# Mixing experts by 32 tokens and 4 slots, with replicated token rows, in a one-core encoder kernel

## The reference, cut to what matters

```
q = (xb @ wq) per head, RMS-normed                  # 8 heads of 256
s1, s2 = q1 @ k1.T, q2 @ k2.T                       # 128 keys each
v1, i1 = top_k(s1, 16);  v2, i2 = top_k(s2, 16)
sv, si = top_k(v1[:, None] + v2[None, :], 16)       # of 256 sums
expert = i1[si // 16] * 128 + i2[si % 16]           # one of 16384
g   = softmax(sv)
act = gelu(sum_d u[expert, d] * xb[d])
out = sum over 8 heads and 16 places of g * act * v[expert]
```

## Time and profile before

| | us |
|---|---|
| median of 3 runs | 3307.72 |
| lowest and highest run | 3305.47, 3307.9 |
| span of the profiled execution | 3302.0 |
| gather stage, first issue to the last mix | 587.3 to 3294.0 |

### The profile page before, as it was taken

The page is one execution under the profiler, slowest core; times in us unless marked ns, Lnnn a source line. Parts: engine busy times, 40 slices in busy tenths (PEclk is TensorE's granted clock), DMA queues, the critical chain, the costliest instruction groups (busy, mean ns, idle before and its releaser), DMA issues. The chain is left out here.

```text
span 3302.0 us, 33384 instructions
## 1 busy us (share of the span) xinstructions
PE 2886.4 (87%) x9454; PEld 1408.2 (43%) x9454; DVE 2218.7 (67%) x5274; ACT 2154.6 (65%) x7216; POOL 1392.2 (42%) x1135
## 2 busy tenths in 40 slices
PE   7999999888888888888898888888988898889886
PEld 5665455444434433444344344343443344434321
DVE  5687265776676667666766676667666766676665
ACT  3332143677777777777777777777777777777775
POOL 0000110455544555554455544544555445544553
PEclk9999999999999999999999999999999999999999
DMA  7232133999999999999999999999999999999997
GB/s 284 87 104 76 30 122 125 369 419 418 420 419 403 419 420 420 414 420 420 420 396 420 420 420 419 420 421 418 403 420 420 420 413 420 420 418 406 421 420 302
DMA packets 170079, 1190.91 MB, mean 361 GB/s; under 512 B 20058, under 2 KB 21498, under 8 KB 30242
## 3 DMA queue, kind: packets, MB, share of 16 engines
q0 software_dynamic: 155808, 1118.53, 82.1%
q1 hardware_dynamic: 14084, 70.23, 5.7%
HBM read 1179.42 MB, written 9.25 MB: 360 GB/s over the span
## 5 line engine op out<-in xcount | busy, mean ns | idle before, releaser
L929 PE MATMUL ps<-r_w,r_yT 128*128 128x512 f32 (+1 forms) x2712 | 1320.6, 622 | 256.2 <-ACT r_yT L1255 253.4
L604 POOL DMA_INDIRECT r_w<-in_peer_uv,gidx x678 | 860.5, 1269 | 880.3 <-PE ps L929 841.8
L1806 DVE SCALAR_TENSOR_TENSOR r_w<-r_w,r_qk 128x1024 f32<-128x1024 f32 x678 | 829.9, 1225 | 499.9 <-DMA r_w<-in_peer_uv,gidx 494.7
L929 PEld LDWEIGHTS ps<-r_w,r_yT 128*128 128x128 f32 (+1 forms) x2712 | 485.8, 192 | 1018.3 <-ACT r_yT L1255 600.8
L929 PE MATMUL ps<-r_yT 128*128 128x512 f32 (+1 forms) x904 | 443.7, 620 | 72.4 <-ACT r_yT L1255 70.1
L1247 ACT ACTIVATE mixc<-mixc 128x1 f32<-128x1 f32 x1056 | 207.8, 197 | 449.5 <-DVE r_w L1806 286.0
L1255 ACT ACTIVATE r_yT<-ident,mixc 128x128 f32<-128x128 f32 x1024 | 411.3, 402 | 33.2
L1252 ACT ACTIVATE mixc<-mixc 128x1 f32<-128x1 f32 x1056 | 408.9, 387 | 35.0
L1251 ACT ACTIVATE mixc<-mixc 128x1 f32<-128x1 f32 x1056 | 408.7, 387 | 33.8
L604 POOL DMA_INDIRECT r_yT<-in_peer_uv,gidx x226 | 298.5, 1321 | 269.4 <-PE ps L929 257.3
L1806 DVE SCALAR_TENSOR_TENSOR r_yT<-r_yT,r_qk 128x1024 f32<-128x1024 f32 x226 | 276.6, 1225 | 176.1 <-DMA r_yT<-in_peer_uv,gidx 175.9
(11 more groups left out here) (293 smaller groups left out, 2777.3 us busy)
## 6 DMA issues: line engine op xcount, KB each, us to landing
r_w<-in_ada_w SPq DMA_DIRECT2D x18, 1024.0 KB, 5.3
r_w<-in_peer_uv,gidx POOLq DMA_INDIRECT x678
r_w<-in_w_lin SPq DMA_DIRECT2D x16, 512.0 KB, 6.9
r_vo<-in_x_prompt SPq DMA_DIRECT2D x8, 512.0 KB, 7.2
r_qk<-in_ada_w SPq DMA_DIRECT2D x2, 2048.0 KB, 16.7
r_w<-in_w_out SPq DMA_DIRECT2D x2, 2048.0 KB, 8.9
r_w<-in_x_prompt SPq DMA_DIRECT2D x8, 512.0 KB, 3.5
x_dram<-r_w POOLq DMA_DIRECT2D x8, 512.0 KB, 3.4
```

The lines of the kernel that those rows point to most:

```text
L604: pool.indirect_dma_start(ring[i], None, table, bass.IndirectOffsetOnAxis(gidx_t[:, h, j:j + 1], 0)).then_inc(e_ld[i], 16)
L929: mm = nc.tensor.matmul(ps[0:r, 2 * p + c, :], diag[:, j % 4, 0:r], row[:, D + c * 512:D + (c + 1) * 512], start=h == 0 and j == 0, stop=h ...
L1806: V.scalar_tensor_tensor(ring[i][:, 0:D], ring[i][:, 0:D], 1.0, h2[:, t, :], ALU.mult, ALU.mult, accum_out=dots[:, i:i + 1]).then_inc(dot_ ...
```

## The change

A slot is now 32 tokens by 4 places of one head instead of 128 tokens by 1 place. The number of gathers (1056), their rows (128) and their size (8 KB) stay.

- Partition group k (of 32) holds place 4g+k of the same 32 tokens. For this the 32 token rows are repeated four times: `replicate` makes them with two matmuls against the constant `spread`, ScalarE copies them from PSUM (`copy_rows`) into one of two buffers `xrep`, and a buffer serves 4, 8 or 16 slots (`SETS`: the heads that are taken together for one group of 32 tokens).
- Places and gates must be moved to the right partitions: VectorE spreads them with a mask (`xi`, `xg`), TensorE sums them (`turn_places`, `turn_gates`, four calls each), VectorE converts the places (`copy_places`), ScalarE copies the gates (`copy_gates`).
- `mix` is four calls, each a diagonal 128x32 against 256 columns of v, into the four column groups of the array; the sum over four places falls out of it. There is one accumulator, so the first mix of a tile waits on `acc_free`.
- `weight` has five instructions instead of six; the factor of the tanh moves into the dot.
- The accumulator is laid out in 4 x 256 columns by 32-partition groups. The final steps therefore work on [128, 4, 256] (for the sample tile on [128, 1, 256]), the sum of squares over the four groups is made on TensorE (`sum_squares`), and x1 and y move in four DMAs each, with rows of 1 KB. The rows g2 and the final weights are loaded in 12 small DMAs.
- The table `ROUTE_AT` says at which slot the routing of each head begins, one head every 16 slots from the seventeenth on; six early heads (`FAST`) are routed in fewer slots.

The diff, cut to its core (the constants, the slots' order, the SyncE transfers of a tile's end, TensorE's new steps, ScalarE's weight, VectorE's places, gates, dot and final sum):

```diff
-K_ROUTE, K_GATE, K_W, K_FIN = 13, 2, 3, 3
+K_ROUTE, K_W, K_FIN = 14, 3, 5
+QUADS, NG = 4, 16
+QC = 256
+SETS = [((0,), (1,), (2, 3), (4, 5), (6, 7)), ((0, 1), (2, 3), (4, 5, 6, 7))] + [
+    ((0, 1, 2, 3), (4, 5, 6, 7))] * (NT - 3) + [((0,), (1,))]
+FAST = (2, 3, 12, 13, 14, 15)
+ROUTE_AT = {2: 2, 3: 10, 4: 22, 5: 37, 6: 53, 7: 69, 8: 85, 9: 101, 10: 116, 11: 132,
+            12: 146, 13: 154, 14: 162, 15: 170, 16: 180}
+ROUTE_AT.update({m: 180 + 16 * (m - 16) for m in range(17, (NT - 1) * HEADS + S_STEPS)})
...
-            return (t, h + 2, P) if h < HEADS - 2 else (t + 1, h + 2 - HEADS, rn)
+        slots, builds, first = [], [], []
+        for t in range(NT):
+            for heads_of in SETS[t]:
+                for q in range(QUADS if t < NT - 1 else 1):
+                    builds.append((t, q))
+                    first.append(len(slots))
+                    for h in heads_of:
+                        for c in range(4 * q, 4 * q + 4) if t < NT - 1 else range(NG):
+                            slots.append((t, h, q, c, len(builds) - 1, number(t, heads_of[-1])))
+        assert len(slots) == N_SLOTS
+        first.append(N_SLOTS)
+        spans = {}
+        for n, x in enumerate(slots):
+            spans.setdefault((x[0], x[2] // 2), []).append(n)
+        N_ROUTES = number(NT - 1, S_STEPS)
+
+        def routes(s):
+
+            return [m for m in range(2, N_ROUTES) if 0 <= s - ROUTE_AT[m] <= 20]
+
+        def build_at(s):
+
...
-            def finish(t, r, src, dst):
-                sp.dma_start(x1s[0:r], src).then_inc(x1_ld, 16)
+
+            def finish(t, nq, src, dst):
+                for c in range(4):
+                    sp.dma_start(x1s[c * DEC:(c + 1) * DEC, 0:nq, :],
+                                 src[:, c * QC:(c + 1) * QC].rearrange("(q j) n -> j q n", q=nq)).then_inc(x1_ld, 16)
                 sp.wait_ge(y_out, t + 1)
-                sp.dma_start(dst, h2[0:r, t, :]).then_inc(y_st, 16)
-
-            for t in range(NT - 2):
-                finish(t, P, x1_t[t], y_t[t])
-            sp.wait_ge(y_st, 16 * (NT - 2))
-            sp.dma_start(g2s, mod_dram[1, 5 * D:6 * D].partition_broadcast(DEC)).then_inc(g2_ld, 16)
-            finish(NT - 2, P, x1_t[NT - 2], y_t[NT - 2])
-            finish(NT - 1, DEC, x1_dram[SEQ:T], outs[1][0])
-            sp.wait_ge(y_st, 16 * NT)
+                for c in range(4):
+                    sp.dma_start(dst[:, c * QC:(c + 1) * QC].rearrange("(q j) n -> j q n", q=nq),
+                                 h2[c * DEC:(c + 1) * DEC, t, 0:nq * QC].rearrange("p (q n) -> p q n", q=nq)).then_inc(y_st, 16)
+
+            for t in range(NT - 1):
...
+            def turn_places(m):
+
+                pe.wait_ge(idx_x, m + 1)
+                if m:
+                    pe.wait_ge(gate_ready, m)
+                for k in range(4):
+                    mm = nc.tensor.matmul(ps[k * DEC:(k + 1) * DEC, 6, 16:32], sel32, xi[:, :, k:NG:4],
+                                          start=True, stop=True)
+                mm.then_inc(idx_t, 1)
+
+            def turn_gates(m):
+
+                pe.wait_ge(gate_x, m + 1)
+                pe.wait_ge(idx_ready, m + 1)
+                for k in range(4):
+                    mm = nc.tensor.matmul(ps[k * DEC:(k + 1) * DEC, 6, 32:48], sel32, xg[:, :, k:NG:4],
+                                          start=True, stop=True)
+                mm.then_inc(gate_t2, 1)
+
+            def replicate(b):
+
+                t, i = builds[b]
+                if b:
+                    pe.wait_ge(x_copy, b)
+                q = slice(i * DEC, (i + 1) * DEC)
                 for c in range(2):
-                    mm = nc.tensor.matmul(ps[0:r, 2 * p + c, :], diag[:, j % 4, 0:r], row[:, D + c * 512:D + (c + 1) * 512],
-                                          start=h == 0 and j == 0, stop=h == steps(r) - 1 and j == TOPK - 1)
+                    mm = nc.tensor.matmul(ps[:, 2 + c, :], spread[q, :],
+                                          h2[q, t, c * 512:(c + 1) * 512], start=True, stop=True)
+                mm.then_inc(x_rep, 1)
+
+            def mix(s):
+
+                t, h, q, _, _, _ = slots[s]
+                pe.wait_ge(dg_ready, s + 1)
+                if t and s == t * TILE_SLOTS:
+                    pe.wait_ge(acc_free, t)
+                row = ring[place[s]]
+                new, end = s == spans[t, q // 2][0], s == spans[t, q // 2][-1]
+                for c in range(4):
+                    mm = nc.tensor.matmul(ps[c * DEC:(c + 1) * DEC, q // 2, (q % 2) * QC:(q % 2 + 1) * QC], diag[:, s % 4, :],
+                                          row[:, D + c * QC:D + (c + 1) * QC], start=new, stop=end)
                 mm.then_inc(v_free, 1)
 
-            pe.wait_ge(kt_ld, 16)
...
-            def weight(t, h, r, j):
-
-                s = slot0(t, h) + j
+            def weight(s):
+
+                t, h, _, c, _, m = slots[s]
                 wch.base, wch.n = s * K_W, 0
-                i, d = j % 2, dots[:, place[s]:place[s] + 1]
+                i, d = s % 2, dots[:, place[s]:place[s] + 1]
+                if s == 0 or m != slots[s - 1][5]:
+                    act.wait_ge(gate_ready, m + 1)
                 act.wait_ge(dot_done, s + 1)
-                nc.scalar.activation(sq[:, i:i + 1], d, ACT.Square, scale=(TANH_K * GELU_C) ** 0.5)
-                act.wait_ge(v_free, s + 5)
-                nc.scalar.activation(kd[:, i:i + 1], d, ACT.Copy, scale=TANH_K)
-                wch.link(nc.scalar.activation(gd[:, i:i + 1], gate_t[:, h, j:j + 1], ACT.Copy, scale=d))
-                wch.link(nc.scalar.activation(th[:, i:i + 1], sq[:, i:i + 1], ACT.Tanh, scale=d, bias=kd[:, i:i + 1]))
+                wch.mark(nc.scalar.activation(sq[:, i:i + 1], d, ACT.Square, scale=GELU_C ** 0.5 / TANH_K))
+                nc.scalar.activation(gd[:, i:i + 1], gate_t[t % 2][:, h, c:c + 1], ACT.Copy, scale=d)
+                wch.need()
+                wch.link(nc.scalar.activation(th[:, i:i + 1], sq[:, i:i + 1], ACT.Tanh, scale=d, bias=d))
                 wch.link(nc.scalar.activation(wc[:, i:i + 1], th[:, i:i + 1], ACT.Identity, scale=gd[:, i:i + 1],
                                               bias=gd[:, i:i + 1]))
                 assert wch.n == K_W
-                nc.scalar.activation(diag[:, j % 4, 0:r], (ident if r == P else sel32)[:, 0:r], ACT.Copy,
+                act.wait_ge(v_free, RING + s - 3)
+                nc.scalar.activation(diag[:, s % 4, :], sel32, ACT.Copy,
                                      scale=wc[:, i:i + 1]).then_inc(dg_ready, 1)
+
+            def copy_gates(m):
+
+                t, h = tile_head(m)
+                act.wait_ge(gate_t2, m + 1)
+                nc.scalar.activation(gate_t[t % 2][:, h, :], ps[:, 6, 32:48], ACT.Copy).then_inc(gate_ready, 1)
+
+            def copy_rows(b):
+
+                act.wait_ge(x_rep, b + 1)
+                if b >= 2:
+                    act.wait_ge(dot_done, first[b - 1])
+                nc.scalar.activation(xrep[b % 2], ps[:, 2:4, :].rearrange("p b n -> p (b n)"), ACT.Copy).then_inc(x_copy, 1)
 
...
                 assert rc.n == K_ROUTE, rc.n
-                V.scalar_tensor_tensor(gidx_t[:, h, :], e12[:, half[0]], float(P), e12[:, half[1]],
-                                       ALU.mult, ALU.add).then_inc(idx_ready, 1)
-
-            def gates(m, h):
-                gc.base, gc.n = m * K_GATE, 0
+                V.tensor_tensor(xi, idxf.unsqueeze(1).broadcast_to([P, QUADS, NG]),
+                                jm.unsqueeze(2).broadcast_to([P, QUADS, NG]), ALU.mult).then_inc(idx_x, 1)
+
+            def copy_places(m):
+                t, h = tile_head(m)
+                dve.wait_ge(idx_t, m + 1)
+                V.tensor_copy(gidx_t[:, t % 2, h, :], ps[:, 6, 16:32]).then_inc(idx_ready, 1)
+
+            def gates(m):
                 dve.wait_ge(p_exp, m + 1)
-                gc.link(V.reciprocal(prs, psm))
-                gc.link(V.tensor_scalar(gate_t[:, h, :], pexp, prs, 0.5, ALU.mult, ALU.mult))
-                assert gc.n == K_GATE
-
-            def dot(t, h, j):
-                s = slot0(t, h) + j
-                i = place[s]
+                link(V.reciprocal(prs, psm))
+                if m:
+                    dve.wait_ge(gate_t2, m)
+                V.scalar_tensor_tensor(xg, pexp.unsqueeze(1).broadcast_to([P, QUADS, NG]), prs,
+                                       jmk.unsqueeze(2).broadcast_to([P, QUADS, NG]), ALU.mult, ALU.mult).then_inc(gate_x, 1)
+
+            def dot(s):
+                i, b = place[s], slots[s][4]
+                if s == first[b]:
+                    dve.wait_ge(x_copy, b + 1)
                 dve.wait_ge(e_ld[i], 16 * uses[s])
-                V.scalar_tensor_tensor(ring[i][:, 0:D], ring[i][:, 0:D], 1.0, h2[:, t, :], ALU.mult, ALU.mult,
+                V.scalar_tensor_tensor(ring[i][:, 0:D], ring[i][:, 0:D], TANH_K, xrep[b % 2], ALU.mult, ALU.mult,
```

(26 more changed lines are left out.)

421 lines of the change are left out of this document (238 added, 183 removed).

## The result

The changed kernel takes 3336.5 us (median of 4 runs, 3334.5 to 3337.8), the kernel before on the same chip 3306.6 (3303.8 to 3307.9): a ratio of 1.009, 95% interval 1.0076 to 1.0104. The forecast was 3309.7 with a range of 3298 to 3333. It missed on the slow side.

The account below looks back on a forecast made before the run. The gather stage was taken to be bound by DMA at 2.485 us per gather, one lagging engine setting the dots. Span 3302.0 - 1.3 + 4 - 2.7 + 2 = 3304.0, plus 5.7 to the median: 3309.7 us, range 3298 to 3333.

Parts of the forecast that it names:

- Step 1: Mixes on four column groups: about 0.6 us or 1.9 as now, below the 2.49 between mixes, so nothing in the stage.
- Step 2: Builds of replicated rows, two TensorE calls and a ScalarE copy per 4 to 16 gathers: hidden, cost 0.
- Step 3: Turning places and gates on TensorE: places reach GpSimd just in time, a miss of some us costs 0.
- the laggard: The one DMA engine that lags and sets the dots in the gather stage; its queue covers 22.8 us with 11 places.
- Rival D: GpSimd waits for late places at each of some 20 set borders, a few us each: 3330 to 3350; chance 0.05.
- Step 4: Program fetches in the gather stage: ScalarE's shrinking program moves the end by -1.3 us, TensorE's growing one costs 0.
- Step 5: Residual and output in 1 KB rows at the eight tile borders: +4 us, from 1.5 to 11.
- Step 6: Chain after the last dot, with smaller VectorE passes and a shorter mix: -2.7 us, from -1.7 to -3.0.
- Step 7: Start of the stage: first dot 6 us later, eleventh gather issued at about 621.5 instead of 618.37: +2 us, 0 to +4.
- A: Dips in the mean DMA share at tile borders do cost, and the shorter mix shrinks them: 3299 us; chance 0.15.
- B: TensorE's program fetches, on only two DMA engines, decide the stage once they grow: 3337 us; chance 0.10.
- C: Short mixes leave TensorE at 1.2 GHz, so queries stop gathers at the first tile borders: +14, 3324 us; chance 0.10.

Follow-up runs that it names:

- e13: Changed kernel with heads taken in pairs in all tiles from 1 on, one head routed every 16 slots: 3329.5 us, ratio 1.0059.
- e9: Kernel before with five ScalarE instructions per weight instead of six, the tanh factor moved into the dot: 3306.4 us, ratio 0.9996.
- e1: Changed kernel with three idle TensorE calls of 256 columns behind each mix: 3443.4 us, ratio 1.042.
- e4: Kernel before with two more TensorE calls of 8 columns behind each mix: 3308.3 us, ratio 1.0006.
- e3: Kernel before with residual load and output store each in four DMAs of 1 KB rows over all 128 partitions: 3309.8 us, ratio 1.0011.
- e11: Kernel before with only the residual's loads in blocks of 32 partitions by four rows of 1 KB, rows permuted: 3324.3 us, ratio 1.005.
- e6: Kernel before with residual loads and output stores in blocks of 32 partitions by four rows of 1 KB, rows permuted: 3324.0 us, ratio 1.0058.
- e15: Changed kernel with e13's pairs and the residual's loads over all 128 partitions in 1 KB rows, rows permuted: 3316.0 us, ratio 1.0024.
- e10: Kernel before with five idle VectorE passes of 1024 columns, about 6.3 us, ahead of the first dot: 3308.2 us, ratio 1.0001.
- e5: Changed kernel with two idle TensorE calls behind each mix, but none next to a query or a build: 3339.0 us, ratio 1.0103.
- e7: Changed kernel with tile 1's sample query moved to head 0 and head 2's routing begun at slot 3 instead of 2: 3332.8 us, ratio 1.0083.
- e12: Changed kernel with tile 1's sample query moved to head 0 and two idle calls behind mixes only in slots 3 to 109: 3332.0 us, ratio 1.0067.

## Why the prediction was wrong, step by step

**What bounds the kernel** was read rightly: the pace stayed at 2.49 us, dots wait for gathers, and the time is in the extras above the pace.

**Step 1, the column groups.** Right. A mix takes 0.64 us at the full clock and 1.08 at half, so the four groups run beside each other. It gained nothing in the stage, as forecast.

**Step 2, the replicated rows.** Held as to time: e13 has 16 builds per tile, twice as many as the changed kernel's later tiles, and is no slower.

**Step 3, places just in time.** This step failed. I checked when a head's places reach GpSimd and priced lateness at nothing, since the laggard's queue covers a few us. I looked at the regular distance of 16 slots, and not at heads 12 to 15, 8 slots apart, one of them (13) with the sample's query besides. There VectorE's wait for the gates takes its dots along (6.7 us at once, 10.0 in two waits), and the queue of 8 places is not deep enough: from 1020 to 1050 the DMA engines fall short. Price: 8.3 us instead of 0, of which e13 gives back 7.5. Rival D has this sign but not this place or size: it put it at every set's border.

**Step 4, the instruction streams.** The size came near by luck; the reason is not borne out. ScalarE's program did not shrink: the 909 activations that went are outweighed by waits that are now instructions of their own (1332 in the trace instead of 174), and the stage has 103 q14 packets, where it had 100 before. In e9, which drops the activation and adds no waits, it has 91. What changed is the size of the steps. Steps of 0.96 us now stand where a q14 packet passes (the queues of 2420 to 2423, and the dots on either side):

```profile
q14 instruction: 1, 0.01, 0.7%
```

```profile
2419.33 1.23 DVE L1934 SCALAR_TENSOR_TENSOR r_w<-r_w,r_vo 128x1024 f32<-128x1024 f32 x1 [0.39 <-DMA r_w<-in_peer_uv,gidx]
...
2422.78 1.23 DVE L1934 SCALAR_TENSOR_TENSOR r_w<-r_w,r_vo 128x1024 f32<-128x1024 f32 x1 [1.73 <-DMA r_w<-in_peer_uv,gidx]
```

They go with VectorE's program. Of the 24 steps of 0.90 to 1.02 us behind slot 60, 22 fall at places 51 to 66 when VectorE's records are counted modulo 128; in the kernel before the 28 steps of 0.62 to 0.75 us fall at places 56 to 82 of ScalarE's. e9 has 24 steps of 0.90 to 1.02 too. Why ScalarE's packets, as many as before, leave hardly a step in the changed kernel is open. And the slots outside the named ranges lose 2.7 us of extra, where I had -1.3, but that is inside the scatter: they have 25.9 here, 25.5 to 32.9 in the variants of the changed kernel (e1 left out), and 28.8 in the kernel before.

TensorE's packets are 99 in the stage (about 100 forecast); e4 shows in the kernel before that 31 more of them cost nothing that shows.

```profile
q8 instruction: 99, 1.62, 0.2%
```

**Step 5, rows of 1 KB.** The term that failed by most: +4 (1.5 to 11) forecast, 17.8 measured at the borders. I costed packet by packet, by size, and the size explains none of the borders: e3 has the same rows and the old borders (its total, +3.4 us, is no more than the +4). What costs is that each load writes into 32 partitions, four rows to each, while gathers run: e11 (loads alone) +16, e6 (loads and stores) +18, e15 (loads over 128 partitions) 13.4 back. By the traces that is 2.1 us (e11) and 2.2 us (e15 against e13) for each of the seven borders with a load of 512 KB; the changed kernel has 2.5 more at each. The earlier trace rows could not show this, for its 4 KB rows lie over 128 partitions. The Trainium skill ("DMA: Bandwidth & Descriptors", Specifications), which I weighed there, puts the line rate at transfers of 512 B and more. e3's borders agree, at 3.2 to 3.9 us extra with rows of 1 KB; that row speaks of size alone and says nothing of a block of 32 partitions.

**Step 6, the tail.** Right: -2.9 against -2.7. The first of the small passes, 0.42 us instead of 1.22:

```profile
3327.78 0.42 DVE L1945 TENSOR_TENSOR r_qk<-ps,r_wr 128x256 f32<-128x256 f32 x1 [2.68 <-PE ps L1000]
```

**Step 7, the start.** This term failed too: +2 forecast, 9.7 measured, 2.2 of it ahead of the first gather, so about 7. The issue behind the third mix comes 6.7 us later, not 3.1; the forecast left out the query that now stands ahead of this mix (6.31 us). But that this issue sets the loss is not borne out. e10 issues the same gather 34.5 us after its first, the changed kernel 35.5 and the kernel before 31.0, and e10 loses nothing; e5 issues at 35.5 as well, and its lateness at slot 16 is 610.9 instead of 614.6; e7 issues at 33.5 and gains nothing. The direct DMAs of 625 to 630 us are in no term of the prediction and in no experiment. The cause of the start's loss stays open. That a late first dot is covered was right (e10).

**The rivals.** A fell with its sign, for the kernel is slower; its premise got no run of its own. B fell by e4. C had its condition right, the clock stands at 0.50 for 78% of the stage, and its price, +14 us, wrong: e15 is only 7.6 us above the kernel before at a clock of 0.68, with the borders and most of tile 1 mended. At the start the clock may play a part.

**The sum of the miss.** On the span I forecast 3304.0, and it is 3333.9, 29.9 more: 13.8 in step 5 (17.8 - 4), 8.3 in step 3, 7.7 at the start (9.7 - 2, of it 2.2 ahead of the stage), 1.7 in slots 30 to 60, less 1.4 in the other slots and 0.2 at the tail. The first is shown by e11 and e15, the second by e13; the start is not explained. On the median the miss is 26.8, for the 5.7 us that I added between span and median is 2.6 in this kernel. The slots from 30 to 60 have no experiment of their own; in e13 and e15 they have 1.7 and 2.0 extra.

## What to carry to other kernels

Where gathers hold all DMA engines, the shape of a direct transfer beside them counts as well as its bytes and its row size: try it over 128 partitions, even if the layout wants blocks of 32 (e15 shows what that gives back, not a kernel with the right output). Look at the densest place of a schedule, not at its rule: four routings at half distance cost 8.3 us here, where the regular ones of e13 leave 2.5 extra against 1.7 before. And read GB/s beside the DMA share: here a share of 1.07 with 299 GB/s was contention, and in e12 a share of 0.71 with 266 GB/s was a queue that ran dry.

## What the runs showed of the hardware

- Loads in blocks of 32 partitions, 512 KB at a time, slow the gathers beside them by 2.1 to 2.2 us (e11, e15), 299 to 365 GB/s at a DMA share of 1.02 to 1.07 (the changed kernel, e11), and a gather's 8 KB packet takes 325 to 328 ns over such a border instead of 315. The same rows of 1 KB over 128 partitions cost nothing at the borders (e3, 406 GB/s, 316 ns) and +3.4 us (0.7 to 6.9) in all. The stores in blocks add nothing that shows (e6 against e11). Why is open: which DMA engines the block's packets go to, and the order of rows in DRAM, were not tried.
- Four matmul groups of 32 columns, 256 wide, take 0.64 us together at the full clock, 1.08 at half, where two of 512 over all columns took 1.92.
- With mixes this short the granted clock is 0.50 for 78% of the stage (mean 0.673 over the whole kernel), and between the gathers, at the borders and in e13's tile 1 this stage, bound by DMA, shows no loss from it.
- Steps that go with VectorE's program, one in some 128 of its instructions, are 0.96 us; those that go with ScalarE's were 0.69 in the kernel before.
